# The second RWKV finish and the odd output projection in one block, four slices of the contraction ahead of the finish

## The reference

```
y_c  = gelu(s5_ssm(u) + d_skip * u);  g_a, g_b = split(y_c @ w_glu)
o_c  = g_a * sigmoid(g_b) * silu(z_c)                  # S5 branch, 512 channels
y    = recurrence of RWKV-7 (r, k, v, decay, a)        # 8 heads of 64
y    = (y - mean) * rsqrt(var + eps) * ln_w + ln_b + bonus   # mean, var over each head's 64
o_d  = y * silu(z_d)                                   # RWKV branch, 512 channels
out  = x + concat(o_c, o_d) @ w_out                    # contraction over 1024
```

## Time and profile before

| | |
|---|---|
| median of 3 runs | 1590.32 us (1588.74 to 1592.79) |
| profiled execution, its own time | 1596.58 us |
| its span, first to last instruction | 1594.8 us |
| PE busy | 1334.8 us (84%) |
| DVE busy | 913.6 us (57%) |
| ACT busy | 457.9 us (29%) |
| POOL busy | 323.9 us (20%) |
| mean granted TensorE clock | 0.884 |

### The profile page before, as it was taken

How to read it: one execution, slowest core, us unless ns; L and a number is a source line. 1 busy time by engine, 2 the same in 40 slices (tenths; PEclk the granted TensorE clock), 3 DMA queues, 4 the chain that set the end, 5 groups by cost and what they waited for, 6 DMA issues and landing times. The chain is left out here.

```text
span 1594.8 us, 20480 instructions
## 1 busy us (share of the span) xinstructions
PE 1334.8 (84%) x8434; PEld 1114.4 (70%) x8434; DVE 913.6 (57%) x1230; ACT 457.9 (29%) x670; POOL 323.9 (20%) x164
## 2 busy tenths in 40 slices
PE   5999999899577959948997999996426799998498
PEld 4777888686466848847886888884214788888387
DVE  5367746710587464158975655844798575364831
ACT  5134343312233241042431212313444212221300
POOL 3222222211056053022221111220203200000420
PEclk9999999899788979989999999998755665899699
DMA  5212122221300031352331426120000000100523
GB/s 176 43 39 62 44 57 80 67 67 41 112 1 1 1 119 56 130 172 80 106 95 48 125 55 178 54 85 34 0 1 1 1 1 1 54 1 1 185 62 123
DMA packets 118709, 101.97 MB, mean 64 GB/s; under 512 B 37144, under 2 KB 102808, under 8 KB 118488
## 3 DMA queue, kind: packets, MB, share of 16 engines
q1 hardware_dynamic: 104984, 81.65, 17.2%
q10 hardware_dynamic: 13632, 19.01, 3.7%
HBM read 74.43 MB, written 24.51 MB: 62 GB/s over the span
## 5 line engine op out<-in xcount | busy, mean ns | idle before, releaser
L167 PE MATMUL banks<-xt_lo,w_hi 128*128 128x512 f32 x816 | 322.7, 395 | 6.5 <-POOL w_lo L488 6.5
L169 PE MATMUL banks<-xt_hi,w_hi 128*128 128x512 f32 x816 | 319.1, 391 | 0.0
L168 PE MATMUL banks<-xt_hi,w_lo 128*128 128x512 f32 x816 | 319.1, 391 | 0.0
L488 POOL TENSOR_TENSOR w_lo<-features,w_hi 128x1024 fp32r<-128x1024 f32 x55 | 149.0, 2710 | 526.8 <-ACT w_hi L497 526.8
L167 PEld LDWEIGHTS banks<-xt_lo,w_hi 128*128 128x128 f32 x816 | 154.2, 189 | 42.0 <-POOL w_lo L488 7.0
L169 PEld LDWEIGHTS banks<-xt_hi,w_hi 128*128 128x128 f32 x816 | 154.0, 189 | 32.5
L168 PEld LDWEIGHTS banks<-xt_hi,w_lo 128*128 128x128 f32 x816 | 154.3, 189 | 31.3
L541 ACT ACTIVATE temporaries<-banks 128x1024 f32<-128x1024 f32 x47 | 56.0, 1192 | 326.8 <-PE banks L169 318.4
L1581 DVE TENSOR_TENSOR temporaries<-temporaries,banks 128x1024 f32<-128x1024 f32 x16 | 19.5, 1221 | 115.0 <-PE banks L169 106.2
L286 PE MATMUL banks<-temporaries,features 128*128 128x128 f32 x256 | 36.5, 304 | 35.2 <-DVE temporaries L263 35.2
L497 ACT ACTIVATE w_hi<-features 128x1024 fp32r<-128x1024 f32 x55 | 57.8, 1054 | 27.9 <-PE banks L169 26.7
(11 more groups left out here) (445 smaller groups left out, 2649.9 us busy)
## 6 DMA issues: line engine op xcount, KB each, us to landing
features<-in_even_w_in SPq DMA_DIRECT2D x26, 512.0 KB, 4.0
features<-in_odd_w_in SPq DMA_DIRECT2D x25, 512.0 KB, 4.7
features<-in_x SPq DMA_DIRECT2D x8, 512.0 KB, 7.9
even_gates<-temporaries ACTq DMA_DIRECT2D x8, 512.0 KB, 2.6
features<-even_gates SPq DMA_DIRECT2D x8, 512.0 KB, 8.8
features<-in_even_w_out SPq DMA_DIRECT2D x8, 512.0 KB, 3.6
temporaries<-in_x SPq DMA_DIRECT2D x8, 512.0 KB, 4.0
h_between_layers<-temporaries SPq DMA_DIRECT2D x8, 512.0 KB, 4.6
```

Source lines behind the costliest of these rows:

```text
L167: nc.tensor.matmul(out, w[0], x[1], start=start, stop=False)
L168: nc.tensor.matmul(out, w[1], x[0], start=False, stop=False)
L169: return nc.tensor.matmul(out, w[0], x[0], start=False, stop=stop)
L488: nc.gpsimd.tensor_tensor(wl[n % 2], wr[n % NW], wh[n % 2].bitcast(F32), ALU.subtract).then_inc(low, 1)
```

## The change

`project_out` no longer builds a block. It returns the five generators, and `side_by_side` makes the block. In the odd layer this block holds the second finish and the projection together:

```diff
-    side_by_side(co, clearing(co), gates_of(co, zg), r7_state(co, second), r7_finish(co, first, gated=(co.gates_in, 64)))
-    w_out = a["odd_w_out"][0]
-    w_in = [co.sem(f"oout_w{i}", kept=True) for i in range(3)]
-    ahead = [(co.at(A_F[4] + 1024 * i, (D,)), w_out[i * P:(i + 1) * P, :], sem) for i, sem in enumerate(w_in)]
-    side_by_side(co, clearing(co), r7_finish(co, second), out_ahead(co, [(zc[b], oc[b]) for b in range(WB)], ahead))
-    project_out(co, "oout", w_out, zc + r,
-                [A_F[2] + 1024 * k for k in range(KT)], [A_F[0] + 1024 * k for k in range(KT)], x, dst, co.output_stored, ahead=w_in)
+    side_by_side(co, clearing(co), gates_of(co, zg), r7_state(co, second), r7_finish(co, first, (co.gates_in, 64), A_BIG, 0, lambda t: 5 + 3.4 * t))
+    side_by_side(co, clearing(co, at=100), r7_finish(co, second, None, A_BIG + 4096, 6, lambda t: t),
+                 project_out(co, "oout", a["odd_w_out"][0], zc + r, [A_F[2] + 1024 * k for k in range(KT)], [A_F[0] + 1024 * k for k in range(KT)], x, dst,
+                             co.output_stored, fetch=[(zc[b], oc[b]) for b in range(WB)], early=WB, ready=(co.finish_done, 2)))
```

Slices 0 to 3 are `early`: their parts and their products for the token tiles 0 to 2 carry numbers that fall between those of the finish. The finish transposes into banks 6 and 7, which belong to tile 3; so tile 3 of the early slices comes after the finish. `ready` is the second of the finish's two final products. The core of the new `project_out`:

```diff
+    base = 20 if early < KT else 0
+
+    def sync(sp):
+        yield 0
+        for k in range(3):
+            if not fetched:
+                sp.dma_start(wr[k], w[k * P:(k + 1) * P, :]).then_inc(loaded[k], 16)
+            if k < len(fetch):
+                sp.dma_start(*fetch[k]).then_inc(mixed_in[k], 16)
+        for k in range(3, len(fetch)):
+            sp.dma_start(*fetch[k]).then_inc(mixed_in[k], 16)
+        for k in range(3):
+            sp.dma_start(rr[k], res[k * P:(k + 1) * P, :]).then_inc(resin[k], 16)
+        for k in range(3, KT):
+            sp.wait_ge(low_w, k - 2)
+            sp.dma_start(wr[k % 3], w[k * P:(k + 1) * P, :]).then_inc(loaded[k % 3], 16)
...
+    def scalar(act):
+        for k in range(KT):
+            yield 5 + 2.5 * k if k < early else base + k
+            if k < len(fetch):
+                act.wait_ge(mixed_in[k], 16)
+            if k == early:
+                act.wait_ge(*ready)
+            nc.scalar.activation(mh[k], mixed[k], ACT.Copy).then_inc(high_m, 1)
+            act.wait_ge(loaded[k % 3], 16 * (k // 3 + 1))
+            nc.scalar.activation(wh[:, k, :], wr[k % 3], ACT.Copy).then_inc(high_w, 1)
+
+    def gpsimd(pool):
+        for k in range(KT):
+            yield 5 + 2.5 * k if k < early else base + k
...
+        for k in range(KT):
+            yield 8 + 3.5 * k if k < early else base + 2 + k
+            if k == early:
+                pe.wait_ge(*ready)
+                for k_ in range(early):
+                    products(3, k_)
+            pe.wait_ge(low_m, k + 1)
+            pe.wait_ge(low_w, k + 1)
+            for t in range(3 if k < early < KT else 4):
+                products(t, k)
+        yield base + 40
+        for t in range(4, NT):
...
+    def vector(dve):
+        for k in range(KT):
+            yield (6, 9.5, 11, 15.5)[k] if k < early < KT else base + k
```

`clearing` gets the place of the semaphores' clearing as an argument: at 100 it comes last on POOL. The even layer calls the same `project_out` with its weights already fetched and nothing early:

```diff
-    project_out(co, "eout", a["even_w_out"][0], v + zb,
-                [A_F[0] + 1024 * k for k in range(KT)], [A_F[2] + 1024 * k for k in range(KT)], x, dst, [co.sem(f"eout_stored{i}", kept=True) for i in range(3)], ahead=w_in)
+    out_stored = [co.sem(f"eout_stored{i}", kept=True) for i in range(3)]
+    side_by_side(co, clearing(co, at=100), project_out(co, "eout", a["even_w_out"][0], v + zb, [A_F[0] + 1024 * k for k in range(KT)], [A_F[2] + 1024 * k for k in range(KT)],
+                                                       x, dst, out_stored, fetched=w_in))
```

More of the change, by code:

```diff
@@ L1504, in _, with project_out @@
                     nc.scalar.activation(pt[n % 2][:, WB * c:WB * c + WB, :], banks(4)[:, WB * c:WB * c + WB, :], ACT.Copy).then_inc(pt_out, 1)
-def project_out(co, tag, w, mixed, hi_at, lo_at, res, dst, stored, ahead=None):
+def project_out(co, tag, w, mixed, hi_at, lo_at, res, dst, stored, fetched=False, fetch=(), early=KT, ready=None):
     nc = co.nc
@@ L1515, in project_out @@
     rr = [co.at(A_T + 1024 * i, (D,)) for i in range(3)]
-    old = co.old_sems()
-    loaded = ahead or [co.sem(f"{tag}_w{i}") for i in range(3)]
+    loaded = fetched or [co.sem(f"{tag}_w{i}") for i in range(3)]
     resin = [co.sem(f"{tag}_r{i}") for i in range(3)]
[L1519 to L1522, removed]
-            for k in range(KT):
[L1524 to L1581, removed]
@@ new lines, in tensor, with products @@
+    def tensor(pe):
+        def products(t, k):
+            ts_ = slice(t * P, (t + 1) * P)
+            for h in range(2):
+                hs = slice(h * 512, (h + 1) * 512)
+                last = three_passes(nc, co.ps[:, 2 * (t % 4) + h, :], (mh[k][:, ts_], ml[k][:, ts_]), (wh[:, k, hs], wl[:, k, hs]), k == 0, k == KT - 1)
+            if k == KT - 1:
+                last.then_inc(multiplied, 1)
+        for k in range(KT):
[10 more added lines that the diff above has]
+        for t in range(4, NT):
+            pe.wait_ge(added, t - 3)
+            for k in range(KT):
+                products(t, k)
@@ new lines, in vector @@
+    def vector(dve):
+        for k in range(KT):
+            yield (6, 9.5, 11, 15.5)[k] if k < early < KT else base + k
+            dve.wait_ge(high_w, k + 1)
+            nc.vector.tensor_tensor(wl[:, k, :], wr[k % 3], wh[:, k, :].bitcast(F32), ALU.subtract).then_inc(low_w, 1)
+        yield base + 40
+        for t in range(NT):
+            dve.wait_ge(multiplied, t + 1)
+            dve.wait_ge(resin[t % 3], 16 * (t // 3 + 1))
+            nc.vector.tensor_tensor(rr[t % 3], rr[t % 3], co.ps[:, 2 * (t % 4):2 * (t % 4) + 2, :].rearrange("p b n -> p (b n)"), ALU.add).then_inc(added, 1)
@@ L1585, in start @@
+    return dict(sync=sync, scalar=scalar, gpsimd=gpsimd, tensor=tensor, vector=vector)
 def start(co):
@@ L2124, in r7_ahead, with clearing @@
         (x.w2a2[0:64, :], a["rwkv_w2"][0]), (x.w2a2[64:128, :], a["rwkv_a2"][0])]
-def clearing(co):
+def clearing(co, at=-2):
     old = co.old_sems()
     def gpsimd(pool):
-        yield -2
+        yield at
         co.clear(pool, old)
@@ L2523, in gates_of, with r7_finish @@
     return dict(sync=sync)
[L2526 to L2541, removed]
+def r7_finish(co, x, gated, at, first_bank, pace):
     nc = co.nc
@@ L2545, in r7_finish @@
     y = x.kk.rearrange("p j (g v) -> p (j g) v", v=64)
-    sq = co.at(A_BIG, (32, 64))
-    yt = [co.at(A_BIG + 2048 + 1024 * j, (T,)) for j in range(2)]
+    sq = co.at(at, (32, 64))
+    yt = [co.at(at + 2048 + 1024 * j, (T,)) for j in range(2)]
     mean, var, rs = (co.at(A_MISC + 680 + 32 * i, (32,)) for i in range(3))
@@ L2568, in vector @@
         for j in range(2):
-            yield 45 + 20 * j
+            yield pace(13 + 4 * j)
             dve.wait_ge(mapped, j + 1)
             link(nc.vector.tensor_tensor(yt[j], yt[j], x.bon[:, j, :], ALU.add))
-            yield 48 + 20 * j
+            yield pace(14 + 4 * j)
             if gated is not None:
@@ L2577, in scalar @@
     def scalar(act):
-        yield 20
+        yield pace(7)
         act.wait_ge(summed, 1)
```

33 lines of the change are left out of this document (23 added, 10 removed).

## The result

| | before | after |
|---|---|---|
| median | 1591.55 us (4 runs) | 1575.97 us (4 runs, 1572.04 to 1576.33) |
| ratio | | 0.9889, 95% interval 0.9856 to 0.9921 |
| profiled execution, its time; span | 1596.58; 1594.8 | 1572.04; 1570.3 |
| R1, first recurrence (from one POOL memset to the next) | 130.25 | 120.81 |
| R2, from there to the finish's first reduction | 89.04 | 85.11 |

The stretches show it.

A forecast was written before the change was run, and what follows sets the result against it. PE bounds the kernel from 1501.6 us on; during the finish before that, a DVE chain, it is mostly idle. 1596.58 - 12.5 - 0.7 = 1583.4, less 6.3 to the median gives 1577.1 us; range 1574.5 to 1583.

The forecast's parts named there:

- The first finish beside the second half's recurrence: Second recurrence: only the places of the first finish's steps move, PE sets the pace; -0.7 us in all.
- The term for the transposes themselves: Second recurrence: first transposes move into PE's idle time ahead of a read, -0.8 us; second ones stay between steps, 0.
- (b): Last block: PE's clock stays at half for early slices and tile 3; +18 us, 1595, slower than before; chance 0.04.
- (d): Second recurrence: moved first finish delays several chunks by 1 to 2 us; gain under 5 us, 1586 to 1590; chance 0.05.
- The new block, 12.5 us: Last block: early products fill PE's idle time during the finish; last add starts at 103.1 instead of 115.6 us.
- The collisions: Last block: POOL's and DVE's subtractions exclude each other, 3.4 us per pair; reductions don't collide, at worst +2.3.
- zc0's landing at 5.1: Start of the last block: tile zc0, issued second, lands 5.1 us after the block's start, 8.0 at the other end.
- The root on ACT with its table load, +0.1: Second recurrence: ACT's root now stands ahead of a copy the next chunk needs; +0.1 us, between 0 and +1.6.
- DVE's moved steps, 0: Second recurrence: the first finish's long DVE operations exchange slots of the same kind; 0, at worst +1.2 us.
- Even projection, 0: Even layer's projection: same instructions in the same order in another wrapper; 0 us.
- From the profile to the median, -6.3: Whole kernel: the profiled execution took 1596.58 us, 6.3 above the median of three runs, so 6.3 is taken off.
- (c): Last block: collisions fall well, normalising product beats ml1, wl1 is ready early, ramp 3.1; -1.6 us, 1575.5; chance 0.09.

The follow-up runs named there:

- the kernel with the first finish only: Kernel before with only the first finish's order numbers changed to the new pace; median 1585.49 us, ratio 0.9958 [0.9933, 0.9983] to the kernel before.

## Why the prediction was wrong

The step that failed is "The first finish beside the second half's recurrence": "I take -0.7 in all". It was -3.9: 85.0 to 85.1 in five profiles with the new place of the first transposes against 89.0 to 89.2 in four with the old one. The term for the transposes themselves was right (-0.8; chunk 10.49 to 9.70, and again 0.86 for the second in its own experiment). What was missing is the last chunk, 10.2 to 7.0 us: the clock falls 81 us behind the block's start when the first transposes stand at 35 and doesn't when they stand at 39. The row of the matmuls at 1466.74, 1.49 us for what takes 1.10 elsewhere, was in the trace, and the forecast did not ask what an 0.8 us shift would do to a clock that falls in the middle of a chunk. No rival covered it: (b) has the clock stay low in the new block, (d) lets the recurrence come out longer, and none lets it come out shorter. Why the clock holds with the shift stays open.

With -3.9 the sum is 12.5 + 3.9 = 16.4 us, a ratio of 0.9897; both measured intervals of the changed kernel hold it, as they hold the 0.9917 of the forecast. That the term was too small is shown by R2 and by the kernel with the first finish only, whose interval excludes 0.7 us, and not by the changed kernel's times.

Point by point:
- *What bounds the kernel*: right. With the early products put behind the finish B is 116.05.
- *The new block, 12.5 us*: right, 12.54. Start 10.75 for 10.95; ramp 5.7 and not 4.0, which cost nothing, since slice 1 was not ready earlier and the 1.15 us of idle time went into it (with a ramp of 3.1 the idle time is 1.26 and B the same). Full clock came between 16.4 and 16.8 and not at 15; last gate 28.2 for 28.5. That the total hits within 0.1 us is in part luck: the 1.7 us that the ramp was off, 0.8 us of PE's time, fell into idle time.
- *The collisions*: right in kind. ml1 won against the normalising product and made it 4.49 us; the second reduction was not held up by POOL (2.29 us beside it), the bound of +2.3 wasn't needed.
- *zc0's landing at 5.1*: its copy began at 4.8.
- *The root on ACT with its table load, +0.1*: right in size. The next read waited for ACT at 1416.36, 0.96 us where 0.92 is usual; with the root at its old place R2 is 0.1 shorter (85.01 for 85.12).
- *DVE's moved steps, 0*: right, by the experiment that left them at their old places (85.01).
- *Even projection, 0*: right. From its first low half on DVE to its last add it takes 92.37 us in both kernels. The block boundary showed no gain of its own (B 116.05 with all work behind the finish).
- *From the profile to the median, -6.3*: this hid something. The profile of before had R1 9.4 us longer than usual. The sum took only differences from it, so no term was hurt, but the table above compares single profiles and its 24.5 us would be read wrongly without the repeats.
- *Rivals*: none came. (b) was about the clock in the wrong block, with the wrong sign. (c)'s 1575.5 lies next to the measured median of 1575.97, but what it rests on did not come: ml1 won, and the ramp was longer than forecast.

## What to carry to other kernels

Give an engine that is the bound of one stage the work of that stage while the stage before leaves it idle, and count the new stage instruction by instruction along each queue: that came out within 0.1 us here, with the luck named above. Where a clock falls inside a stretch that is to be moved, cost the move twice, with the fall and without it; a shift of 0.8 us was worth 3.9 to 4.0. And before an operation is moved back in one queue, look at what the other queues have ordered around it.

## What the runs showed that was not expected

- The clock's steps keep their distance from the start of R2, whatever came before: up between 16 and 17 us behind it in all fourteen profiles and, in five, down between 81 and 82 us, though R1 took 116.7, 120.8 or 130.3 us.
- R1, 1072 matmuls with the same code, takes 120.8 us at a granted clock of 0.74 in twelve of the fourteen profiles, and 116.7 (0.81) and 130.3 (0.67) in one each.
- With a wait of 1.73 instead of 0.52 us in the last chunk the fall came back, the last three chunks starting at the same places, and R2 was 4.7 us longer.
